# A mixture-of-experts stage walked from four places, with weights fetched only where the expert changes, a split-precision first product, and the residual parked in DRAM

## The reference, cut to what matters

```python
def expert_block(args):
    tok_b, w_b, e = args
    xb = h[tok_b]
    y = (jax.nn.silu(xb @ w_gate[e]) * (xb @ w_up[e])) @ w_down[e]
    return y.astype(F32) * w_b[:, None]
y_rows = lax.map(expert_block, (row_tok.reshape(n_blocks, EXPERT_BLOCK),
                                row_w.reshape(n_blocks, EXPERT_BLOCK), block_e))
return jnp.zeros((T, D), F32).at[row_tok].add(y_rows.reshape(n_rows, D))
```

## Time and profile before

| what | value |
|---|---|
| median of 3 runs | 4588.61 us (4587.88 to 4592.49) |
| span of the profiled execution | 4588.3 us |
| TensorE matmul busy | 4012.9 us, 87% |
| VectorE busy | 1813.7 us, 40% |
| ScalarE busy | 1251.6 us, 27% |
| POOL busy | 797.8 us, 17% |
| DMA moved | 795.22 MB, mean 173 GB/s |

### The profile page before, as it was taken

One profiled execution on the slowest core, in us unless ns is written; L12 is line 12 of the kernel. 1 busy time (PEld: TensorE's weight loads), 2 busy tenths in 40 slices (PEclk: granted clock), 3 DMA queues, 4 the chain that ended last, 5 costly groups with the idle time before them and its releaser, 6 DMA issues. The chain is left out here.

```text
span 4588.3 us, 75257 instructions
## 1 busy us (share of the span) xinstructions
PE 4012.9 (87%) x29716; PEld 2689.6 (59%) x29716; DVE 1813.7 (40%) x2469; ACT 1251.6 (27%) x1779; POOL 797.8 (17%) x586
## 2 busy tenths in 40 slices
PE   6999888887969998888879888887989999999953
PEld 3888666665747886666657645434544444444423
DVE  3355554554760005555537616523411111111128
ACT  1111254442331112444423325302011111111104
POOL 2122112111332221131114200000010000000024
PEclk8999998987989999999889999997999999999975
DMA  6775333113414423332124226101089999999967
GB/s 219 215 227 178 122 112 127 53 41 114 138 67 147 139 96 120 106 126 64 39 92 137 83 74 258 40 31 73 1 332 356 360 361 355 358 357 360 358 234 264
DMA packets 293693, 795.22 MB, mean 173 GB/s; under 512 B 29889, under 2 KB 121538, under 8 KB 257602
## 3 DMA queue, kind: packets, MB, share of 16 engines
q1 hardware_dynamic: 245346, 616.41, 38.7%
q10 hardware_dynamic: 25632, 93.33, 5.0%
q0 software_dynamic: 22464, 81.80, 4.9%
HBM read 622.64 MB, written 160.43 MB: 171 GB/s over the span
## 5 line engine op out<-in xcount | busy, mean ns | idle before, releaser
L463 PE MATMUL ps<-s_proj_hS,s_proj_wS 128*128 128x512 f32 x3216 | 768.5, 401 | 62.9 <-POOL s_proj_wS L353 62.9
L463 PEld LDWEIGHTS ps<-s_proj_hS,s_proj_wS 128*128 128x128 f32 x3216 | 614.9, 192 | 212.6 <-ACT s_proj_wS L413 63.7
L518 PE MATMUL ps<-gate_h,gate_w 128*128 128x512 f32 x1536 | 415.1, 422 | 35.4 <-PEq L146 19.3
L518 PEld LDWEIGHTS ps<-gate_h,gate_w 128*128 128x128 f32 x1536 | 293.8, 196 | 138.0 <-issue 52.1
L3220 PE MATMUL ps<-s_exp_gu,keep_hT 128*128 128x512 f32 x736 | 340.7, 606 | 15.9 <-DMA s_exp_gu<-in_w_gu_dram 13.9
L3204 PE MATMUL ps<-s_exp_wd,s_exp_aT 128*128 128x512 f32 x736 | 332.8, 595 | 1.9 <-ACT s_exp_aT L3130 1.9
L3225 PE MATMUL ps<-s_exp_gu,keep_hT 128*128 128x512 f32 x736 | 330.9, 592 | 0.0
L505 POOL TENSOR_TENSOR gate_w<-gate_raw,gate_w 128x512 fp32r<-128x512 f32 x128 | 185.1, 1448 | 822.8 <-ACT gate_w L499 822.0
L3170 DVE TENSOR_TENSOR s_exp_sg<-s_exp_sg,ps 128x256 f32<-128x256 f32 x92 | 38.7, 421 | 663.2 <-ACT s_exp_sg L3151 663.2
L381 DVE COPY s_proj_o<-ps 128x512 f32<-128x512 f32 x66 | 45.6, 690 | 570.2 <-PE ps L463 570.2
L353 POOL TENSOR_TENSOR s_proj_wS<-s_proj_w,s_proj_wS 128x1024 fp32r<-128x1024 f32 x67 | 170.5, 2547 | 568.7 <-ACT s_proj_wS L413 568.7
(11 more groups left out here) (453 smaller groups left out, 6095.5 us busy)
## 6 DMA issues: line engine op xcount, KB each, us to landing
s_exp_gu<-in_w_gu_dram SPq DMA_DIRECT2D x184, 1024.0 KB
s_exp_wd<-in_w_down_dram SPq DMA_DIRECT2D x92, 1024.0 KB
yrow<-keep_hT ACTq DMA_DIRECT2D x92, 512.0 KB
keep_mix<-in_w_ada_dram SPq DMA_DIRECT2D x80, 512.0 KB, 6.9
s_proj_w<-in_w_in_dram SPq DMA_DIRECT2D x66, 512.0 KB
proj<-s_proj_o ACTq DMA_DIRECT2D x66, 512.0 KB
gate_raw<-in_w_in_dram SPq DMA_DIRECT2D x128, 256.0 KB, 3.5
yrow<-keep_xT SPq DMA_DIRECT2D x4, 8192.0 KB, 49.2
```

Source lines behind the costliest of these rows:

```text
L463: mm = pe.matmul(k.ps[:, 6 + half if last else 2 * b + half, :], wS[:, b, x, t, :], hS[:, y, t, half * HALF:(half + 1) * HALF], start=(t = ...
L518: mm = pe.matmul(self.k.ps[:, self.banks[g // 2], :], weight[:, w, t - t0, :], self.k.hG[:, h, t, :], start=(t == 0 and w + h == 0), stop= ...
```

## The change

- The used blocks, rounded up to a multiple of four, are cut into four equal runs, and a round takes one block of each run (`starts`), so that block `i` of stream `u` follows block `i - 1` of the same stream. There is a set of weight buffers for each of the four streams: `gu0`, `wd0` and `wd1` lie where the residual `k.xT` was.
- POOL fetches the weights with indirect DMAs, one index per partition. `k.widx[:, 0]` holds the row of each block's expert, `k.widx[:, 1]` the same plus `FAR` where the block has the expert of the one before; with a bound and `oob_is_err=False` an index past the bound is to be left out. Round 0 uses the first list, later rounds the second.
- The gate and up product is made from split parts: ScalarE makes the high parts of the rows and of the weights (`wS`, in four pairs of row tiles), VectorE the low parts, TensorE does three F32R matmuls for each of the eight row tiles. The down product stays float32.
- ScalarE copies the whole output, SP stores it. The residual is stored to DRAM in `route` and read back by SP in the last round.
- `route` ends with six small VectorE operations that make `k.widx`.

```diff
-NR = NBLK // 2
+STREAMS = 4
...
 
-    final = eng.snap(eng.value_load(k.nr[0:1, 0:1], min_val=0, max_val=NR - NE // 2) + (NE // 2 - 1))
-    yield 0, False
-    yield 1, False
-    with eng.Fori(2, NR - 1) as i:
+    final = eng.snap(eng.value_load(k.nr[0:1, 0:1], min_val=0, max_val=(NBLK - NE) // STREAMS) + (NE // STREAMS - 1))
+    one = eng.snap(final + 1)
+    two = eng.snap(one + one)
+    starts = (0, one, two, eng.snap(two + one))
+    yield 0, False, starts
+    yield 1, False, starts
+    with eng.Fori(2, NBLK // STREAMS - 1) as i:
         with eng.If(i < final):
-            yield i, False
-    yield final, True
+            yield i, False, starts
+    yield final, True, starts
...
+            for t in range(KT):
+                sp.dma_start(k.scratch["x1"][t], k.xT[:, t]).then_inc(st_x, 16)
...
             sp.wait_ge(st_eb, 16)
-            sp.dma_start(k.eb[:], ebd.rearrange("p o -> o p")).then_inc(ld_back, 16)
-            sp.wait_ge(ld_back, 16)
+            sp.dma_start(eball[:], ebd.rearrange("p o -> o p").to_broadcast([P, NBLK])).then_inc(ld_back, 16)
+            sp.wait_ge(st_x, 16 * KT)
...
+            dve.wait_ge(ld_back, 16)
+            mine.do(dve.tensor_copy(ebw[:, 0], eball[:]))
+            mine.mark(dve.memset(same[:], 0.0))
+            mine.do(dve.tensor_scalar(ebw[:, 1], ebw[:, 0], float(P), pidx[:, 0:1], ALU.mult, ALU.add))
+            mine.mark(dve.tensor_copy(k.widx[:, 0], ebw[:, 1]))
+            tt(same[:, 1:NBLK], ebw[:, 0, 1:NBLK], ebw[:, 0, 0:NBLK - 1], ALU.is_equal)
+            mine.do(dve.scalar_tensor_tensor(k.widx[:, 1], same[:], float(FAR), ebw[:, 1], ALU.mult, ALU.add))
...
-        gu, wd = s.sb("gu", [P, 2, KT, 2 * DE]), s.sb("wd", [P, 2, 2, D])
-        x, y = k.hT2[:, 0:2], k.hT2[:, 4:6]
-        xT = k.hT2[:, 2:4].rearrange("p u (t n) -> p u t n", t=KT)
-        idx = s.sb("idx", [P, 2], I32)
+        gu = [k.gu0] + [s.sb(f"gu{u}", [P, KT, 2 * DE]) for u in range(1, STREAMS)]
+        wd = k.wd0 + [s.sb(f"wd{u}", [P, 2, D]) for u in range(2, STREAMS)]
+        wS = s.sb("wS", [P, PR, 2, 2, 2 * DE], F32R)
...
         @block.sync
         def _(sp):
-            for i, last in used_rounds(sp, k):
-                for u in range(2):
...
-                    wait(sp, gu_half, b - 1)
-                    sp.dma_start(gu[:, u, 0:KH], I["w_gu"][e, :, 0:KH]).then_inc(ld_ga[u], 16)
-                    if isinstance(b, int) and b == 0:
-                        sp.wait_ge(ld_x[0], 16)
...
-                    sp.dma_start(gu[:, u, KH:KT], I["w_gu"][e, :, KH:KT]).then_inc(ld_gb[u], 16)
-                    wait(sp, down_ready, b - 1)
-                    sp.dma_start(wd[:, u], I["w_down"][e]).then_inc(ld_wd[u], 16)
+            for i, last, starts in used_rounds(sp, k):
+                for u in range(STREAMS):
+                    wait(sp, y_taken, i * STREAMS + (u + 1))
+                    sp.dma_start(yrow[:, bass.ds(i + starts[u], 1), :], y[:, u % 2:u % 2 + 1, :]).then_inc(st_y[u % 2], 16)
+                    if last and u == 1:
...
+                        wait(sp, down_ready, i * STREAMS + 2)
+                        for t in range(KT):
+                            sp.dma_start(k.xT[:, t], k.scratch["x1"][t]).then_inc(ld_res, 16)
+            sp.wait_ge(ld_res, 16 * KT)
...
+            def rows(i, u, starts):
+                wait(pool, ld_x[u % 2], i * (8 * STREAMS) + 16 * (u // 2), 16)
+                wait(pool, xtr_ready, i * STREAMS + (u - 1))
+                settled(pool.tensor_copy(idx[:, u % 2:u % 2 + 1], k.idx[:, bass.ds(i + starts[u], 1)]))
+                pool.indirect_dma_start(x[:, u % 2, :], None, hrow, bass.IndirectOffsetOnAxis(ap=idx[:, u % 2:u % 2 + 1], axis=0))\
+                    .then_inc(ld_x[u % 2], 16)
...
+            def fetch(dst, at, src, landed):
+                pool.indirect_dma_start(dst, None, src, bass.IndirectOffsetOnAxis(ap=at, axis=0), bounds_check=bound, oob_is_err=False)\
+                    .then_inc(landed, 16)
+            def gate_up(i, u, starts):
+                wait(pool, ld_gu[u], i * 16, 16)
+                wait(pool, lo_ready, i * (STREAMS * PR) + (PR * (u + 1) - STREAMS * PR))
+                settled(pool.tensor_copy(widx[:, u:u + 1], k.widx[:, 0 if isinstance(i, int) and i == 0 else 1, bass.ds(i + starts[u], 1)]))
+                fetch(gu[u][:].rearrange("p k n -> p (k n)"), widx[:, u:u + 1], w_gu, ld_gu[u])
...
+            def down(i, u, starts):
+                wait(pool, ld_wd[u], i * 16, 16)
+                wait(pool, down_ready, i * STREAMS + (u + 1 - STREAMS))
...
+            for i, last, starts in used_rounds(pool, k):
+                if isinstance(i, int) and i == 0:
+                    rows(0, 0, starts)
+                    gate_up(0, 0, starts)
+                    rows(0, 1, starts)
+                    for u in range(1, STREAMS):
+                        gate_up(0, u, starts)
+                        down(0, u - 1, starts)
+                    rows(0, 2, starts)
+                for u in range(STREAMS):
+                    if not last:
+                        gate_up(i + 1, u, starts)
+                    if not (last and u):
+                        rows(*after(i, u, 3), starts)
+                        down(*after(i, u, 3), starts)
...
+            def high(j, i, u, pr):
+                if pr == 0:
+                    wait(act, ld_gu[u], i * 16 + 16, 16)
+                wait(act, pair_done, j * PR + (pr + 1 - PR))
+                act.activation(wS[:, pr, 0], gu[u][:, 2 * pr:2 * pr + 2], ACT.Copy).then_inc(hi_ready, 1)
...
+            for i, last, starts in used_rounds(act, k):
+                for u in range(STREAMS):
...
+                    if not (isinstance(i, int) and j < 2):
+                        output(j - 2, *after(i - 1, u, STREAMS - 2))
+                    if more:
+                        rows_high(j + 1, *after(i, u, 1))
+                    if not first(i, u):
+                        turned(j - 1)
+                    for pr in range(PR):
+                        if pr == PR - 1:
+                            wait(act, pair_done, j * PR + PR)
+                            wait(act, act_ready, j - 1)
+                            act.activation(sg[:, u % 2], k.ps[:, 2 if u % 2 == 0 else 6, 0:DE], ACT.Sigmoid).then_inc(sg_ready, 1)
+                        if more:
+                            high(j + 1, *after(i, u, 1), pr)
...
+            def low(j, u, pr):
+                wait(dve, hi_ready, j * PR + (pr + 1))
+                dve.tensor_tensor(wS[:, pr, 1], gu[u][:, 2 * pr:2 * pr + 2], wS[:, pr, 0], ALU.subtract).then_inc(lo_ready, 1)
...
+            for i, last, starts in used_rounds(dve, k):
+                for u in range(STREAMS):
...
+                    if more:
+                        rows_low(j + 1, (u + 1) % STREAMS)
+                    for pr in range(PR):
...
+                        if more:
+                            low(j + 1, (u + 1) % STREAMS, pr)
...
+            def gate_up(j, u):
+                wait(pe, xhi_ready, j + 1)
+                wait(pe, xlo_ready, j + 1)
+                wait(pe, act_ready, j - 1)
+                for pr in range(PR):
+                    wait(pe, lo_ready, j * PR + (pr + 1))
+                    for t in range(2):
+                        for h, w in TERMS:
+                            mm = pe.matmul(k.ps[:, 2 if u % 2 == 0 else 6, :], xS[:, u % 2, h, 2 * pr + t, :], wS[:, pr, w, t, :],
+                                           start=(pr == 0 and t == 0 and h + w == 0), stop=(pr == PR - 1 and t == 1 and h == 1))
+                    mm.then_inc(pair_done, 1)
...
+            for i, last, starts in used_rounds(pe, k):
+                for u in range(STREAMS):
+                    j = i * STREAMS + u
+                    if not (last and u == STREAMS - 1):
+                        turn_x(j + 1, *after(i, u, 1))
+                    if not first(i, u):
+                        turn_a(j - 1, (u - 1) % STREAMS)
+                    gate_up(j, u)
+                    if not first(i, u):
+                        down(j - 1, *after(i - 1, u, STREAMS - 1))
+            turn_a(j, STREAMS - 1)
+            down(j, i, STREAMS - 1)
```

More of the change, by code:

```diff
@@ L124, in second_block @@
         self.hT2 = self.keep("hT2", [P, KT, T])
+        at_hT2 = self.nc.sbuf_base - KT * T * 4
+        self.xS = self.nc.alloc_sbuf_tensor_at("exp_x", [P, 2, 2, KT, P], F32R, offset=at_hT2 + 4 * T * 4)
+        self.gu0 = self.nc.alloc_sbuf_tensor_at("exp_gu0", [P, KT, 2 * DE], F32, offset=self.at_xT)
+        self.wd0 = [self.nc.alloc_sbuf_tensor_at(f"exp_wd{u}", [P, 2, D], F32, offset=self.at_xT + (4 + 2 * u) * T * 4) for u in range(2)]
         self.idx = self.keep("idx", [P, P], I32)
-        self.eb = self.keep("eb", [1, P], I32)
+        self.widx = self.keep("widx", [P, 2, P], I32)
         self.nr = self.keep("nr", [1, 1], I32)
@@ L3143, in _ @@
-            turned(act, 0, 0, 0, put, xt_act)
-            for i, last in used_rounds(act, k):
```

(20 more changed lines are left out.)

189 lines of the change are left out of this document (83 added, 106 removed).

## The result

The changed kernel takes 4445.88 us (median of 4 runs, 4437.18 to 4450.87) against 4589.42 of the kernel before on the same chip (4 runs, 4587.88 to 4592.49): ratio 0.9687, 95% interval 0.9675 to 0.9699. The forecast of 4469 was 23 us too high; the time lies in its range. The profiled execution has a span of 4449.1 us.

A forecast was written before the change was run, and what follows sets the result against it. DMA, at 11.72 us a block, was taken as the bound before, TensorE at 10.17 after. From 4588.3 us: blocks -139.5, start +24, loop turns -4.4, copy +0.4 give 4469; range 4430 to 4545.

The forecast's parts named there:

- DMA is the bound, TensorE is 0.16 us behind it.: Expert blocks before the change: transfers take 11.72 us a block, TensorE's own work 11.56; removing bytes alone gains only 15 us.
- The two edits have to be taken together: Expert blocks: skipping weight fetches and the split F32R product were said to need each other for the gain.
- fewer bytes: Expert blocks: 64 weight fetches instead of 92, 298 MB at 358 GB/s, 832 us for the stage, 9.0 us a block.
- TensorE's 10.17: Expert blocks after the change: TensorE's work per block, 11.56 - 6.87 + 5.48 = 10.17 us, range 9.97 to 10.45.
- fetches not left out: Rival, expert blocks: an index past the bound still costs its transfer, 11.72 us a block stays, 4608 us; chance 8%.
- The product.: Gate and up product: 24 F32R matmuls at 0.2285 us, 5.48 us a block instead of 6.87.
- The start.: First round: the third block's row gather queues behind 13.1 MB on POOL, delaying the second product: +24 us, other end 0.
- The gap before the last round: Before the last round: fewer failing loop turns shrink the 8.70 us gap to 4.3, a gain of 4.4 us.
- The end.: End of the expert stage: wider final copy, 1.02 us instead of 0.60, +0.4; reading back the residual 0, 12 without cover.
- The rivals on POOL and VectorE: Expert blocks: POOL's issue time binds, 4509 us (12%) or 5020 (3%); VectorE's low parts slow down and bind, 4545 (9%).

The follow-up runs named there:

- e10: The kernel before, loading 3.15 MB a block instead of 4.19 from its third round on (sums of other weights): 4558.84 us, ratio 0.9933.
- e2: The changed kernel with eight full float32 matmuls on the high parts instead of 24 F32R ones, fetches still left out: 4562.27 us, ratio 0.9941.
- e8: The changed kernel without the product's third term (16 matmuls instead of 24) and with every block fetching its weights: 4415.97 us, ratio 0.9624.
- e1: The changed kernel with every block fetching its weights, 92 fetches instead of 64: 4450.94 us, ratio 0.97.
- e4: The changed kernel with every block fetching its weights and eight full float32 matmuls on the high parts: 4566.59 us, ratio 0.9951.
- e11: The changed kernel with all of POOL's first-round issues written in the order of need: 4437.43 us, ratio 0.9671.

## Why the prediction was right and where it was wrong

- **"DMA is the bound, TensorE is 0.16 us behind it."** The first half held (e10). The second was mis-sized: I took one block's 11.84 less its idle 0.28, but 0.16 more of it lay between the turn of the activations and the product (0.38 us beside the idle 0.28, where e10 has 0.22). TensorE's own block is 11.39 (e2, e10), so removing bytes alone is worth 29 us, not 15.
- **"The two edits have to be taken together"**, with the fewer bytes priced at 358 GB/s. This step failed as far as the fewer bytes go. 358 was no ceiling of the chip but 4.19 MB over the period of a kernel that moved them unevenly; the ceiling is 427 (e8), under which 92 fetches fit in 10.11 us (e1). A DMA share of 0.97 misled me: it says that something was outstanding, not that the rate was full (e4 has 0.96 at 368 GB/s, e1 1.01 at 415). The check lay in the same trace: 419 and 261 GB/s in the two halves of one block. The total survived because I named TensorE's 10.17 as the bound after the change anyway. The rival "fetches not left out" had 4608 for what measured 4451: it would have been no loss at all. What the product depends on is the other way of fetching, if anything, and I had given that no price.
- **The product.** 24 x 0.2285 = 5.48 was predicted, 5.67 came (0.236 each). The rest of the block was put at 4.69 and is 4.44: the next product starts 0.14 us behind the turn of the activations, against 0.22 to 0.66 before. The two errors cancel to 0.06 us a block, or 5.5 us in all; that it is so little is luck.
- **The start.** Predicted +24 from a queue served in order behind 13.1 MB, measured +20.0. The hole was 13.60 us where some 15 was said, ended by the row gather as said, and e11 removes it by order alone. So the mechanism held; two of its terms did not. Of the 24, 21 lay ahead of the second product and 3 in it, for a cold clock; the product took 6.15 us from its start to the down product against 5.67 in the next block, so 0.5. And 36.6 us for 13.1 MB took 358 GB/s again. From 3330 to 3366 the core moved 401 GB/s, 14.4 MB, so more than the counted bytes had gone by when TensorE went on. The higher rate and the further bytes cancel, which is luck.
- **The gap before the last round.** I scaled 8.70 down to 4.3 by the number of loop turns; it is 1.51. The rows do not show why; the scaling was a guess. Nor did the term hold what the cold clock cost there, 1.7 us before and 0.02 after, so that -4.4 became -8.9.
- **The end.** +0.4 for the wider copy, measured -3.3. The last block's product is 1.2 us shorter, the last down product 1.7 (3.67 against 5.37 [4290.81 above, and 4429.37 of before]) and the stretch between them 0.6. Reading the residual back (issued at 4281.84) lies beside the last blocks, at no cost that the table shows.
- **The rivals on POOL and VectorE.** POOL's issues cost the same for 16 KB rows as for 8 KB (below), and VectorE's low parts took 1.225 us at the median and 1.303 at most, as alone. Neither came.

The misses add up to the 19.7 us between the two sums of the table, and all but the last row's point the same way. So the total is not right by cancellation between its rows; cancellation there is inside the terms of the product and the start.

## What to carry to other kernels

A rate that equals bytes over period is what was asked for, not what can be had: cut one period into pieces before calling it a ceiling, and look for stretches of several microseconds that are faster. In a queue served in order, a small transfer behind large ones that nobody needs yet is a wait; write the first round in the order of need, whole, since moving one gather only names the next. When two edits are argued to need each other, undo each alone: here the skipping was worth nothing at this pace and 86 us at the next. And look in the order of issue for a load that stands behind a wait that it does not need.
